# A two-stream block kernel on one core: the second layer's first gated network taken for both streams in matmuls of 512 columns, shorter pauses in two norms, one activation table moved

## What is computed

```
h  = half_ffn(h,  m,  0, g[0], g[1], ffn_w_in[i, 0], ffn_w_out[i, 0])
hc = half_ffn(hc, mc, 0, g[0], g[1], ffn_w_in[i, 0], ffn_w_out[i, 0])
...
swiglu(h) = (silu(h @ w_gate) * (h @ w_up)) @ w_down
```

## Time and profile before

| | us |
|---|---|
| median of 3 runs | 2663.43 (2663.36 to 2664.72) |
| the profiled execution | 2662.17 |
| its span from the first to the last instruction | 2660.4 |
| PE busy | 2509.0 (94%) |
| DVE busy | 1643.9 (62%) |
| ACT busy | 1249.6 (47%) |
| mean granted TensorE clock | 0.977 |

### The profile page before, as it was taken

One profiled execution on the slowest core, in us unless ns is written; L12 is line 12 of the kernel. 1 busy time (PEld: TensorE's weight loads), 2 busy tenths in 40 slices (PEclk: granted clock), 3 DMA queues, 4 the chain that ended last, 5 costly groups with the idle time before them and its releaser, 6 DMA issues.

```text
span 2660.4 us, 48901 instructions
## 1 busy us (share of the span) xinstructions
PE 2509.0 (94%) x20876; PEld 2378.0 (89%) x20876; DVE 1643.9 (62%) x2721; ACT 1249.6 (47%) x1697; POOL 1.2 (0%) x6
## 2 busy tenths in 40 slices
PE   6899998999999999999888999999999999798998
PEld 6799987888999999988787999999999999766998
DVE  5745575566766455656767667576565558656555
ACT  5444453444444444444545555454444345435443
POOL 0000000000000000000000000000000000000000
PEclk9899999999999999999899999999999999898999
DMA  6366656334456665554352345455545555364453
GB/s 224 143 246 242 255 190 216 133 112 154 180 207 237 218 241 179 221 203 178 130 185 87 126 143 175 172 181 175 187 175 184 181 175 190 118 225 157 175 183 119
DMA packets 71591, 480.14 MB, mean 180 GB/s; under 512 B 8784, under 2 KB 9296, under 8 KB 17744
## 3 DMA queue, kind: packets, MB, share of 16 engines
q1 hardware_dynamic: 66240, 468.74, 49.5%
q10 hardware_dynamic: 5136, 8.28, 1.0%
HBM read 471.48 MB, written 1.05 MB: 178 GB/s over the span
## 4 chain that ended last, share of the span: by engine, by line
PE 73%; DVE 14%; ACT 7%; issue 3%; DMA 3%; ACTq 1%; DVEq 0%; SPq 0%
PE bank L267 64%; ACT whi L224 4%; DVE wlo L246 2%; DVE wlo L233 2%; PE bank L1162 2%; DMA raw<-w_main 1%; PE bank L1045 1%; DMA raw<-w_down 1%; PE bank L983 1%; DVE HX L676 1%; DVE ARX L732 1%; DVE tmpx L670 1%; PE bank L1033 1%; DMA tmpx<-ARX 0%; PE bank L1728 0%
## 5 line engine op out<-in xcount | busy, mean ns | idle before, releaser
L267 PE MATMUL bank<-HNX_hi,whi 128*128 128x256 f32 x2968 | 858.6, 290 | 43.5 <-DVE wlo L246 16.8
L233 DVE TENSOR_TENSOR wlo<-raw,whi 128x1024 fp32r<-128x1024 f32 (+1 forms) x378 | 453.3, 1199 | 682.5 <-ACT whi L224 681.9
L224 ACT ACTIVATE whi<-raw 128x2048 fp32r<-128x2048 f32 (+1 forms) x378 | 705.5, 1868 | 313.0 <-PE bank L267 157.6
L267 PE MATMUL bank<-HNX_hi,wlo 128*128 128x256 f32 x2968 | 843.8, 285 | 0.0
L267 PE MATMUL bank<-HNX_lo,whi 128*128 128x256 f32 x2968 | 830.3, 285 | 0.0
L267 PEld LDWEIGHTS bank<-HNX_hi,whi 128*128 128x128 f32 x2968 | 576.5, 194 | 68.4 <-issue 37.8
L267 PEld LDWEIGHTS bank<-HNX_hi,wlo 128*128 128x128 f32 x2968 | 577.1, 194 | 0.0
L267 PEld LDWEIGHTS bank<-HNX_lo,whi 128*128 128x128 f32 x2968 | 568.7, 194 | 0.7 <-issue 0.5
L246 DVE TENSOR_TENSOR wlo<-raw,whi 128x1024 fp32r<-128x1024 f32 (+1 forms) x378 | 450.9, 1193 | 0.0
L267 PE MATMUL bank<-HNC_hi,whi 128*128 128x256 f32 x1344 | 392.0, 292 | 11.6 <-DVE tmpc L482 4.5
L267 PE MATMUL bank<-HNC_lo,whi 128*128 128x256 f32 x1344 | 382.7, 285 | 0.0
(11 more groups left out here) (350 smaller groups left out, 2734.6 us busy)
## 6 DMA issues: line engine op xcount, KB each, us to landing
raw<-w_main SPq DMA_DIRECT2D x270, 1024.0 KB, 4.8
raw<-w_ada SPq DMA_DIRECT2D x72, 1024.0 KB, 4.8
raw<-w_down SPq DMA_DIRECT2D x72, 1024.0 KB, 5.0
raw<-w_down SPq DMA_DIRECT2D x36, 768.0 KB, 4.3
raw<-w_cmp SPq DMA_DIRECT2D x4, 1024.0 KB, 5.4
tmpx<-ARX ACTq DMA_DIRECT2D x18, 128.0 KB, 5.2
tmpx<-ARX ACTq DMA_DIRECT2D x32, 64.0 KB, 4.7
HX<-x_in SPq DMA_DIRECT2D x2, 512.0 KB, 6.0
```

The lines of the kernel that those rows point to most:

```text
L224: NS.activation(WHI[q % HIS][:, 0:size], RAW[m % SLOTS][:, 0:size], ACT.Copy).then_inc(sems["w_hi"], 1)
L233: NV.tensor_tensor(WLO[m % SLOTS][:, 0:half], RAW[m % SLOTS][:, 0:half], WHI[q % HIS][:, 0:half].bitcast(fp32), SUB)
L267: return NT.matmul(dst, (WHI[ordinal[n] % HIS], WLO[n % SLOTS])[w][:, k * 2 * P + col:k * 2 * P + col + P], x[xp][:, kx, :], start=start, ...
```

## The change

1. **Network 4 for both sequences.** The inputs and gated tiles of x and c are laid into one tensor, `BOTH`, so that one access pattern reads the tile of x and the tile of c as 2 x 256 columns. c computes pairs 0 to 3 by itself as before (8 blocks and 4 down blocks, in its own lane) and then stops. x computes its pairs 0 to 3 by itself. Pairs 4 to 10 and their down products are computed once for both, in matmuls of 512 columns into one bank for each output tile: 14 gate and up blocks, 4 down blocks of 6 tiles, 4 of 8 tiles. The order on TensorE is: x's pair 0; pairs 4 to 7; the down blocks of pairs 4 to 6; pairs 8 to 10; x's pair 1; the down blocks of pairs 7 to 10, which finish c; x's pairs 2 and 3; x's own down blocks, 4 of 8 tiles. The gate goes through Tanh. c's norm starts when c is finished, in the last eight blocks of x.
2. **Pitch.** In c's norms before network 3 and before `ga_in` the pause between two tiles is 2.5 in place of 6.0. The one before network 4 keeps 6.0.
3. **The root's table.** The dummy operation that loads the Sqrt table stood ahead of the last two tiles' `put_out`; now it stands behind all of them, at the start of every norm of x that has such sums.

```diff
@@ -97,17 +97,22 @@
+        AX_HN, AX_G = 2 * KD * T, 2 * KF * T
+        AX_ALL, AC_ALL = AX_HN + AX_G + KD * T, 16 * T + KD * T
...
+            ARC = g.enter_context(nc.sbuf_tensor("ARC", [P, AC_ALL], fp32))
+        BOTH = sb("BOTH", [P, AX_ALL + AX_HN + AC_ALL], f32r)
+
...
 
+        def of_both(at_x, at_c):
+
+            whole = BOTH[:, :]
+            return bass.AP(tensor=whole.tensor, offset=whole.offset + at_x, ap=[list(whole.ap[0]), [at_c - at_x, 2], [1, T]])
+
+        def normed_of_both(xp, k):
+            return of_both((xp * KD + k) * T, AX_ALL + (xp * KD + k) * T)
+
+        def gated_of_both(xp, x_slot, c_slot):
+
+            at_c = AX_ALL + AX_HN + (8 * xp + c_slot) * T if c_slot < 8 else AX_HN + (KF * xp + c_slot + 10) * T
+            return of_both(AX_HN + (KF * xp + x_slot) * T, at_c)
+
         def program(pe=None, act=None, dve=None, pool=None, sp=None):
 
@@ -262,26 +280,26 @@
-            def product(dst, n, col, k, x, xp, kx, w, start, stop, loose=False):
+            def product(dst, n, col, k, x, xp, kx, w, start, stop, loose=False, both=None):
 
                 return NT.matmul(dst, (WHI[ordinal[n] % HIS], WLO[n % SLOTS])[w][:, k * 2 * P + col:k * 2 * P + col + P],
-                                 x[xp][:, kx, :], start=start, stop=stop, skip_group_check=loose)
...
 
                     def job(banks=banks, at_n=at_n, at=at, tile=tile, tiles=tiles):
                         if gain is not None:
-                            if not S.lag and at + 2 == KD:
-                                table_of(ACT.Sqrt, 127)
                             for m in range(2):
                                 src = banks[m][:, 0:T] if not S.lag else halves(banks[m])[m]
@@ -435,11 +451,11 @@
-            def ffn(S, which, gain, first):
+            def ffn(S, which, gain, first, parts=None):
 
 
                 t, base, lo_marks = S.tag, MAIN[f"gu{which}"], {}
-                chunks = [range(0, 4), range(4, 8), range(8, 11)] if S.chunked else [range(0, 11)]
+                chunks = parts or ([range(0, 4), range(4, 8), range(8, 11)] if S.chunked else [range(0, 11)])
...
                                 waits = {k: [lo_marks[k // 2]] for k in range(k0, k1) if k % 2 == 0} if mp == 0 else None
                                 tile = up(f"{t}_tile") if cc == 2 else None
                                 yield from two_tiles(S, n, [b[:, 0:T] for b in banks], S.G, ks, cc == 0, cc == 2, waits, tile, 2, mp == 3 and cc == 2)
-                            if mp == 3:
-                                table_of(ACT.Sqrt, 127)
                             for m in range(2):
                                 free[banks[m].name] = put_out(S, banks[m][:, 0:T], 2 * mp + m, gain, done(n) if m else tile)
                         continue
-                    k0, k1 = CHUNKS[c]
+                    k0, k1 = 2 * pairs[0], 2 * pairs[-1] + 2
                     for mp in range(4):
@@ -546,16 +560,187 @@
-                            dst = y if c == 1 else S.TMP[0][:, :]
+                            dst = y if c == 1 or parts else S.TMP[0][:, :]
                             free[bank.name] = ev = up("dve_step")
                             if on(dve, done(n), held["y", mp], held.get("tmp") if c == 2 else None):
                                 NV.tensor_tensor(dst, y, bank[:, :], ADD).then_inc(ev.sem, 1)
                             held["y", mp] = ev
-                            if c == 2:
+                            if c == 2 and not parts:
                                 for m in range(2):
                                     held["tmp"] = put_out(S, S.TMP[0][:, m * T:(m + 1) * T], 2 * mp + m, gain, ev)
                         after(S, partial)
+                if parts:
+                    summed_c.update({mp: held["y", mp] for mp in range(4)})
+                    passed.add(f"c_at{which}")
+                    while f"both{which}" not in passed:
+                        yield ("W",)
+
+            summed_c = {}
+
+            def ffn_of_both(which, gain_x, gain_c, first, alone, groups):
+
+
+                base, held, lows, lo_marks, x_slot, c_slot = MAIN[f"gu{which}"], {}, [], {}, {}, {}
+                GATES, UPS = (BANK[0], BANK[1]), (BANK[2], BANK[3])
+                for m in range(2):
+                    x_slot.update({m: m, 2 + m: 16 + m, **{2 * p + m: 2 * p - 2 + m for p in range(2, alone)}})
+                for j, k in enumerate(range(2 * alone, KF)):
+                    x_slot[k], c_slot[k] = 2 + j, j % 12
+
...
+                def silu(banks, kept, ready):
+
+                    flush()
+                    for bank, tmp, mark in zip(banks, kept, ready):
+                        th, read = up("x_tanh"), up("x_gate_read")
+                        if on(act, mark, held.get(tmp.name)):
+                            NS.activation(tmp[:, :], bank[:, :], ACT.Tanh, scale=0.5).then_inc(th.sem, 1)
+                        if dve:
+                            dve.wait_ge(*th)
+                            NV.scalar_tensor_tensor(tmp[:, :], tmp[:, :], 1.0, bank[:, :], ADD, MUL).then_inc(read.sem, 1)
+                        free[bank.name] = held["read", tmp.name] = read
+
+                def keep(banks, kept, ready, dsts):
+
+                    for bank, tmp, mark, (ks, g_hi, g_lo) in zip(banks, kept, ready, dsts):
+                        ud, hi, lo = up("x_up_done"), up("x_g_hi"), up("x_g_lo")
+                        if on(dve, mark, held["read", tmp.name]):
+                            NV.scalar_tensor_tensor(tmp[:, :], tmp[:, :], 0.5, bank[:, :], MUL, MUL).then_inc(ud.sem, 1)
+                        free[bank.name] = ud
...
+                            NS.activation(g_hi, src, ACT.Copy).then_inc(hi.sem, 1)
...
+                def x_pair(p):
+
+                    gate, up_ = X.pair
+                    for b, bank in enumerate((gate, up_)):
+                        yield ("D",)
+                        n = take("x", "w_main", base + 2 * p + b)
...
+                def both_pair(p):
+
+                    kept = (TMPC, TMPX)[(p - alone) % 2]
+                    for b, banks in enumerate((GATES, UPS)):
+                        yield ("D",)
+                        n = take("x", "w_main", base + 2 * p + b)
+                        on(pe, *(free.get(bank.name) for bank in banks))
+                        tile = up("x_tile")
+                        yield from two_tiles(X, n, [bank[:, :].rearrange("p (a b) -> p a b", a=2) for bank in banks], None, ALL, True, True,
+                                             None, tile, both=normed_of_both)
+                        if b == 0:
+                            silu(banks, kept, (tile, done(n)))
+                        else:
+                            keep(banks, kept, (tile, done(n)), both_tiles(p))
+
+                def down(k0, k1, mp, banks, dsts, x, slots, both=None, behind=()):
+
+                    cuts = (k0, k1) if k1 - k0 <= 8 else (k0, (k0 + k1) // 2, k1)
+                    for a, b in zip(cuts, cuts[1:]):
+                        yield ("D",)
+                        n = take("x", "w_down", (4 * which + mp, a * 2 * P), (b - a) * 2 * P)
+                        if a == k0:
+                            on(pe, *(free.get(bank.name) for bank in banks))
+                        waits = {slots[k]: [lo_marks[k]] for k in range(a, b)} if mp == 0 else None
+                        tile = up("x_tile") if b == k1 else None
+                        yield from two_tiles(X, n, dsts, x, [(k - a, slots[k]) for k in range(a, b)], a == k0, b == k1, waits, tile, both=both)
...
+                def both_down(pairs, opening, closing):
+
+                    k0, k1 = 2 * pairs[0], 2 * pairs[-1] + 2
+                    same = {k: k for k in range(k0, k1)}
+                    for mp in range(4):
+                        banks = (GATES, UPS)[mp % 2]
+                        ready = yield from down(k0, k1, mp, banks, [bank[:, :].rearrange("p (a b) -> p a b", a=2) for bank in banks], None, same,
+                                                lambda xp, k: gated_of_both(xp, x_slot[k], c_slot[k]))
+                        for m, (bank, mark) in enumerate(zip(banks, ready)):
+                            k, copied, added = 2 * mp + m, up("act_step") if opening else None, up("dve_step")
+                            if opening:
+                                if on(act, mark, *free.get(("x", "dst"), ())):
+                                    NS.activation(X.Y[:, k, :], bank[:, 0:T], ACT.Copy).then_inc(copied.sem, 1)
+                                if dve:
+                                    dve.wait_ge(*copied)
+                                    dve.wait_ge(*summed_c[mp])
+                                    NV.tensor_tensor(C.Y[:, k, :], C.Y[:, k, :], bank[:, T:2 * T], ADD).then_inc(added.sem, 1)
+                            elif dve:
+                                dve.wait_ge(*mark)
+                                dve.wait_ge(*held["y", k])
```

(59 more changed lines are left out.)

60 lines of the change are left out of this document (45 added, 15 removed).

## The result

The change makes the kernel **slower**, by 0.6%: 2678.53 us median (2676.85 to 2679.59, 4 runs) against 2663.39 (2656.36 to 2664.72, 4 runs), ratio 1.006, 95% interval 1.0046 to 1.0075. Beside later variants it gave 2678.17 against 2661.38, ratio 1.0055 (1.004 to 1.0069), so 16.8 us by the medians and 14.6 by the ratio. In what follows differences are of medians, and the intervals beside them those of the ratios. One execution of a later variant (`b_pitch_net3`) took 3993.86 us at a granted clock of 0.56 and is left out of its numbers. The forecast was 2656.1, the range 2640 to 2672; the result lies outside. The profiled execution took 2677.94 us, with a span of 2676.2.

What follows compares the result with a forecast made beforehand. The prediction took TensorE's stream as the bound, 94% busy, through network 4. Its terms summed to -7.3 us, carried from the median 2663.4 to 2656.1, with a range of 2640 to 2672.

Steps and rivals of the forecast that it cites:

- part 5: x's norm behind network 4 gains -7.0 us; VectorE's lateness in x's last eight blocks costs +4.0.
- the slack of 7.3: Three buffers of `whi` let the weight split run 7.3 us ahead, taking most of VectorE's lateness in short-pitch norms.
- Part 1: Network 4's shared pairs: 1008 wide matmuls at 227.5 ns gain -12.6 us; fewer loads and splits -1.0.
- Rival A: Wide matmuls in network 4 run at the bare rate, 215 ns, twice the gain: 2643.5 us; chance 0.14.
- B: Wide matmuls in network 4 gain nothing from width, 240 ns: 2668.7 us; chance 0.12.
- Part 2: Hand-overs of banks in network 4's shared pairs and down blocks make TensorE wait: +3.2 us (1 to 5).
- Parts 3 and 4: Short pitch ahead of network 3: -10.3 us; c's early start then costs +3.0 and +11.4 further on.
- the empty norm: x's norm ahead of network 4 stands without c's blocks, 15.4 us in place of 4.3: +11.4.
- Rival D: Lanes move otherwise than counted; the norm ahead of network 4 keeps its five blocks: 2644.7 us; chance 0.12.
- Part 6: The root's table load, moved behind the last sums, delays the root in four empty norms: +2.0 us (0 to 4).
- Rival C: VectorE bounds both short-pitch norms, ScalarE waits behind it and the whole lateness shows: 2673.4 us; chance 0.14.

Runs made afterwards that it cites:

- b_pitch_net3: The kernel before with pitch 2.5 in c's norm ahead of network 3 alone, nothing else: 2653.54 us, ratio 0.9973.
- a_best: The kernel after with pitch 6.0 in both norms of c, x's sum on TensorE and the root's table ahead of the last copies: 2663.41 us, ratio 1.0002.

## Why the prediction was wrong

**The failing step is part 5**, x's last blocks of network 4 and the norm behind them: -7.0 for the norm and +4.0 for VectorE. By the trace of after the blocks took 18.6 us more than before (64.7 against 46.1) in place of 4.0, and the norm 27.0 us in place of the 18.5 that the term was made from. Those two are 23 us, about the whole miss of 22.4.

The row at hand was the pace of x's sums where ScalarE reads a bank, 1.47 us a tile; I added 0.34 for the add and took 1.81. That prices each operation and not the round trip, and the operations too low. The new operation stands ahead of ScalarE's squares and behind VectorE's sums, so each tile pays a whole pass through both queues: 2.50 us, of which 2.0 are work and 0.48 a wait. Then I let "the slack of 7.3" take most of the lateness. It was not there: ScalarE, which fills that slack, stood behind c's norm (13.7 us between two splits). In x's last eight blocks TensorE waited 8.9 and 3.1 us, and most of the other 6.6 are the slower clock behind each wait and c's own sums. The first wait is c's norm at short pitch (8.94 with it, 1.12 without); the second, and the third of 5.5 us in the norm, go with the closing (3.07 and 5.47 with the add on VectorE, 0.44 and 0.73 without). By the runs the closing costs 10 us net of the matmuls that replace it.

**The norm behind network 4** has c's four half blocks in the slots that the forecast gave them, 3 and 1. But it takes 27.0 us with 11.5 of work in them, so 15.5 are lost, where 7.0 were forecast and 14.5 lost before. x's sums start at 2301.83, 15.8 us behind the last down matmul in place of 8.8. Ahead of them c's second block waited 5.47 us for ScalarE's copy L445, which stood behind x's last closing (its add starts at 2291.59), the load of the table and a split of weights. With the add off VectorE the norm takes 21.0, so 9.5 are lost. There is a slip in the working as well: 8.8, 2.9, 3.9 and 2.5 are 18.1 and not 18.5, and 7.0 idle with 3.9 in place of 18.4 are -7.5 and not -7.0.

**Part 1 held.** 227 ns a matmul, 14.4 us by the run with narrow halves against 12.6. Rival A (215 ns; 2643.5) and B (240 ns; 2668.7) are out by the row. The Trainium skill ("TensorE: Matmul & The Clock Gate", Back-to-back issue gap) gives 216 ns for 512 columns, as the gap of a matmul taken by itself; the trace has 227, some 11 ns more, as it was at 256.

**Part 2** held: 3.9 measured against 3.2, in two places of 2.31 and 0.83 us, and none seen at x's own down blocks, where 1.0 had been put.

**Parts 3 and 4** held in sum: +4.1 forecast and about +5.3 measured, and without the empty norm -7.3 and -7.6. Within them the picture was looser, so that the sums agree is in part luck. The empty norm is as drawn, but shorter: from x's last down matmul (1951.7) to its first new one 9.4 us, where 12.0 had been taken. In front of the attention two of x's projection blocks waited 2.36 and 6.11 us for ScalarE's copy (L445), in whose queue c's norm now stands, where I had taken 1.0 off each. Rival D is out.

**Part 6** was small: +2.0 forecast, 3.4 and 4.5 measured, both with intervals that hold 2 and also no change. At 2461 us the root starts 1.88 us behind the start of the last copy, before 1.29: 0.6 more.

```profile
2460.18 0.47 ACT L389 ACTIVATE ARX<-bank,GA 128x256 f32<-128x256 f32 x1
2460.66 1.28 ACT L758 ACT_TABLE_LOAD   x1
2461.95 0.20 ACT L758 ACTIVATE SMALL<-VEC 128x1 f32<-128x1 f32 x1
2462.06 0.30 ACT L750 ACTIVATE sqx<-bank,VEC 128x64 f32<-128x64 f32 x1
```

There is no drain of 1.38 us here either, so the 2.66 us of the Trainium skill ("ScalarE: Activation LUTs", What ACT_TABLE_LOAD costs) do not show in this row: from the start of the load to the root it is 1.40. What would make the whole cost more than 0.6 an empty norm, if it does, is open.

**Rival C** had the right mechanism: it wanted VectorE to bound both norms and gave 2673.4. Ahead of network 3 it shows in part: the waits of 2.36 and 6.11 us are 7.0 more than the usual 0.73 each, where the forecast had charged 5.0 and C 12.3. Behind network 4 it gave the largest wait; but the loss there is not c's norm alone, and VectorE was held up in its queue more than it was full (47.9 busy of 64.7). It had a chance of 0.14, since I weighed it by the number of operations and did not draw the queues of one block.

The books: wide -14.4, banks +3.9, pitch ahead of network 3 with the empty norm +5.3, table some +4.5, closing +10, pitch behind network 4 +3 make 12.3 of 16.8. The remaining 4.5 us were not isolated. They are not the wait of 3.98 us in x's norm that a_best shows, since after has no such wait there; what its trace offers is the first wait, of which 6.25 us are left with the closing eased. Nor are the books exact: the fixes do not add up (about 23 singly, 14.8 together), the last term is within the noise, and the intervals of the ratios are 2 to 4 us to either side. The version that joins the best of both (2653.5 by one number in the old kernel, 2654.8 with three fixes in the new one) was not found: the pitch ahead of network 3 needs c's gates in x's norm, and the wide pass takes them.

## What to carry to other kernels

When an operation of one engine is put between two of another, price the loop of one tile through both queues, not the sum of the operations: from add to add it was 2.50 us with 2.0 of work in it, where 1.81 had been reckoned. Ask of every slack which engine builds it and whether that engine stands in front of a wait in the same stretch. And time a change's parts one by one: one number (the pitch ahead of network 3) was worth 7.6 us by itself, and the rest of the change turned it into a loss of about 5.

## What the runs showed of the hardware

An fp32r matmul whose 512 moving columns come from two separate runs of 256 in one buffer takes 227 ns, against 120 for 256: 107 ns for the second run, which is what the earlier trace rows give for 256 columns, so nothing is left for the step between them (no run here has 512 columns in one run to compare with). Summing on TensorE by an fp32 identity matmul of 256 columns costs 0.37 us a tile at a granted clock of 1.00 (a_best, at 2263.30); over eight tiles it gave 10 us net in this place. And stalls cost twice: in the stretch with waits of 3.1 and 5.5 us, behind one of 8.9, the granted clock was 0.82, against 1.00 with the blocks back to back, and a half block of 24 matmuls took 4.3 us (2297.53 to 2301.83) in place of 2.88.
